# Linear attention of a two-layer step: two output pieces ahead of tile 0, three levels copied by ScalarE, decode preparation on GpSimd

## The reference

```python
def step(S, inp):                       # one chunk of tokens
    qb, kb, vb, gb = inp
    b = jnp.cumsum(gb, axis=2)
    o_inter = jnp.einsum('bhtk,bhkv->bhtv', qb * jnp.exp(b), S)
    decay = jnp.exp(jnp.where(causal, b[:, :, :, None, :] - b[:, :, None, :, :], -jnp.inf))
    att = jnp.einsum('bhtsk,bhsk->bhts', qb[:, :, :, None, :] * decay, kb)
    o_intra = jnp.einsum('bhts,bhsv->bhtv', att, vb)
    b_last = b[:, :, -1:, :]
    S = jnp.exp(b_last[:, :, 0, :])[..., None] * S + jnp.einsum('bhsk,bhsv->bhkv', kb * jnp.exp(b_last - b), vb)
    return S, o_inter + o_intra
...
y = jnp.concatenate([ya, yb, yc], axis=-1) @ lw['w_out']
```

## Time and profile before

| | us |
|---|---|
| median of 3 runs | 2597.96 (2595.11 to 2601.43) |
| the profiled execution, its own time | 2599.04 |
| span of the profiled execution | 2597.2 |
| stage 3 of the first layer, 423.97 to 522.60 | 98.6 |
| stage 3 of the second layer, 1717.80 to 1816.35 | 98.6 |

### The profile page before, as it was taken

One profiled execution on the slowest core, in us unless ns is written; L12 is line 12 of the kernel. 1 busy time (PEld: TensorE's weight loads), 2 busy tenths in 40 slices (PEclk: granted clock), 3 DMA queues, 4 the chain that ended last, 5 costly groups with the idle time before them and its releaser, 6 DMA issues.

```text
span 2597.2 us, 38234 instructions
## 1 busy us (share of the span) xinstructions
PE 2401.4 (92%) x15944; PEld 1422.5 (55%) x15944; DVE 1143.3 (44%) x2122; ACT 689.8 (27%) x1452; POOL 468.2 (18%) x566
## 2 busy tenths in 40 slices
PE   8999998899999999999899999888989999999984
PEld 5645556666666765333366445566666676733332
DVE  3355556843241445333253555568431433633334
ACT  1034444432111331111130344544321123311113
POOL 6004223410100001111260042243100000011112
PEclk9999999999999999999999999999999999999996
DMA  5001001152224228999840010011522421589996
GB/s 187 11 19 30 11 5 38 42 197 92 89 90 148 82 90 310 396 422 422 333 141 11 19 30 11 5 38 44 205 82 65 149 82 65 198 345 406 424 418 244
DMA packets 79220, 389.31 MB, mean 150 GB/s; under 512 B 20654, under 2 KB 24364, under 8 KB 59532
## 3 DMA queue, kind: packets, MB, share of 16 engines
q1 hardware_dynamic: 60892, 308.07, 31.1%
q0 software_dynamic: 17568, 76.57, 7.6%
q10 hardware_dynamic: 576, 2.10, 0.2%
HBM read 354.53 MB, written 41.41 MB: 152 GB/s over the span
## 4 chain that ended last, share of the span: by engine, by line
PE 73%; DVE 11%; ACT 4%; issue 4%; DMA 3%; PEld 2%; POOL 1%; POOLq 0%; PEldq 0%; SPq 0%; DVEq 0%; ACTq 0%
PE ps L1494 12%; PE ps L784 8%; PE ps L807 8%; PE ps L1518 6%; PE ps L1404 4%; PE ps L875 4%; PE ps L955 4%; PE ps L967 3%; PE ps L983 2%; PEld ps L807 2%; PE ps L1160 2%; PE ps L933 2%; DVE arena L2239 2%; PE ps L1480 2%; DMA arena<-yrow 1%
## 5 line engine op out<-in xcount | busy, mean ns | idle before, releaser
L1494 PE MATMUL ps<-arena 128*32 128x512 f32 x2304 | 319.6, 608 | 24.6 <-issue 18.9
L807 PE MATMUL ps<-arena,ring 128*128 128x352 f32 x936 | 283.2, 466 | 1.0 <-ACTq L481 1.0
L784 PE MATMUL ps<-x,ring 128*128 128x352 f32 x768 | 231.5, 463 | 10.6 <-DMA x<-in_x 9.1
L807 PEld LDWEIGHTS ps<-arena,ring 128*128 128x128 f32 x936 | 180.4, 193 | 101.9 <-issue 4.3
L2683 DVE COPY arena<-ps 128x1024 f32<-128x1024 f32 x44 | 53.9, 1224 | 336.9 <-PE ps L1480 336.9
L1494 PEld LDWEIGHTS ps<-arena 128*32 128x32 f32 x2304 | 92.7, 112 | 191.4 <-issue 191.4
L784 PEld LDWEIGHTS ps<-x,ring 128*128 128x128 f32 x768 | 146.8, 192 | 92.7 <-issue 12.8
L1518 PE MATMUL ps<-arena 128*32 128x512 f32 x1408 | 160.2, 595 | 3.8 <-ACT arena L1914 3.8
L2883 POOL DMA_INDIRECT arena<-xrow,arena x46 | 46.8, 1017 | 594.8 <-DVE arena L2658 321.3
L955 PE MATMUL ps<-arena 96*128 96x512 f32 (+3 forms) x384 | 148.7, 497 | 0.0
L1680 ACT ACTIVATE ring<-ps 128x512 f32<-128x512 f32 (+2 forms) x192 | 87.3, 490 | 128.7 <-PE ps L967 128.6
(11 more groups left out here) (471 smaller groups left out, 3836.3 us busy)
## 6 DMA issues: line engine op xcount, KB each, us to landing
arena<-in_w_gu SPq DMA_DIRECT2D x52, 2048.0 KB, 14.3
arena<-in_w_dn SPq DMA_DIRECT2D x64, 1024.0 KB, 11.4
ring<-in_ring SPq DMA_DIRECT2D x56, 512.0 KB, 3.7
ring<-in_w_gu SPq DMA_DIRECT2D x12, 2048.0 KB, 13.7
arena<-yrow SPq DMA_DIRECT2D x16, 1024.0 KB, 9.3
arena<-in_mem_k SPq DMA_DIRECT2D x16, 512.0 KB, 7.6
arena<-in_mem_v SPq DMA_DIRECT2D x16, 512.0 KB, 9.5
xrow<-arena SPq DMA_DIRECT2D x16, 512.0 KB, 7.7
```

Source lines behind the costliest of these rows:

```text
L784: mm = pe.matmul(ps[:, PIECE_BANKS[n % len(PIECE_BANKS)], 0:CH], ring[:, j % RING, k, :], x[:, k, tok], start=k == 0, stop=k == KT - 1)
L807: mm = pe.matmul(ps[:, (j % 2) * NCH + c, 0:CH], ring[:, j // per, (j % per) * units + k, :], src[:, k, tok], start=k == k0, stop=k == uni ...
L1494: mm = pe.matmul(ps[r, 2 + n % 2, :], xb_t[:, n % 2, k, r], w_gu[e % NW][:, k, :], start=k == 0, stop=k == KT - 1, skip_group_check=True)
```

## The change

- **Parts.** Part 0 and part 1 both stand ahead of `levels(0)`. Their weights (both use ring 1) come into a buffer of their own, `w_first`, loaded in stage 2. Part 2 stands between `levels(0)` and `levels(1)`, parts 3 to 7 in tiles 0, 1, 2, 3 and 5. The `keep_clock` of 10 and of 14 go; that of 12 stays.
- **Levels.** DVE's `take_levels` takes the levels 8, 4, 2 and 1 by COPY_PREDICATED. The levels 64, 32 and 16 are plain rectangles, and ACT copies them in seven instructions (`keep_levels`: one, two and four), after `at_free`; then it counts `at_kept`, for which PE's `levels(n + 1)` and `outputs(n)` wait too.
- **State.** `states(n)` makes four products, one a head, so that bank 7 holds only what belongs to the state (cleared once ahead of tile 0), and `add_state` has one instruction in place of two. The turned keys go to the other half of the bank.
- **Start.** DVE runs `begin(2)` ahead of tile 0, once POOL has done the first part of tile 0 (`g_pool` 1), and then `add_part(0)` and `add_part(1)`. ACT runs `decay_exps(2)` there too.
- **Decode tokens.** The running sum, differences, keys and queries are made by POOL behind its tile 7, in buffers of their own; ACT's four exponentials for them stand in tile 7, ahead of `head_squares(7)`. The first cache load comes behind them. DVE's block goes.

```diff
+PART_AT = (0, 1, 2, 3, 5)
...
+                sp.wait_ge(tp_done, SLOT[PAIRS - 2, ("a", 1, 0)] + 1)
+                sp.dma_start(w_first, ins["ring"][l, 2 * RING + PART[0][0]][:, 0:PART_K, :]).then_inc(w_full[0], 16)
...
                     if n >= 1:
                         pe.wait_ge(at_free, n)
+                        pe.wait_ge(at_kept, n)
...
                     pe.wait_ge(kt_evac, n + 1)
-                    pe.matmul(ps[:, 7, 0:GW], g_ktt[:, n % 2, :], vg[:, n, 0:GW], start=True, stop=True).then_inc(st_done, 1)
+                    for h in range(GH):
+                        r, v = slice(GK * h, GK * (h + 1)), slice(GV * h, GV * (h + 1))
+                        mm = pe.matmul(ps[r, 7, v], g_ktt[:, n % 2, r], vg[:, n, v], start=True, stop=True)
+                    mm.then_inc(st_done, 1)
...
-                    pe.wait_ge(ring_full[j], ring_count(l, 3))
+                    if i <= 1:
+                        pe.wait_ge(w_full[0], 16 * (PAIRS // 2 + 1))
+                    else:
+                        pe.wait_ge(ring_full[j], ring_count(l, 3))
                     if i >= 1:
                         pe.wait_ge(part_or_counts_ready, i)
...
-                keep_clock(5, 10)
                 part(0)
+                part(1)
                 levels(0)
-                part(1)
+                part(2)
...
-                    if n == 0:
-                        pe.wait_ge(part_or_counts_ready, 2)
-                        keep_clock(5, 14)
-                    if 1 <= n <= len(PART) - 3:
-                        part(1 + n)
+                    if n in PART_AT:
+                        part(3 + PART_AT.index(n))
...
+                def keep_levels(n):
+
+                    act.wait_ge(at_free, n + 1)
+                    for lv, z in enumerate(LEVELS[:HIGH]):
+                        for b in range(HALF // z):
+                            s_, at = 2 * z * b, lv * HALF + z * b
+                            last = act.activation(g_att[s_:s_ + z, n % 2, :, s_ + z:s_ + 2 * z], ps[s_:s_ + z, 0:GH, at:at + z], ACT.Copy)
...
-                    for lv, z in enumerate(LEVELS):
+                    for lv, z in list(enumerate(LEVELS))[HIGH:]:
...
-                    step(dve.tensor_tensor(g_tmp, ps[:, bank, 0:GW], bd, ALU.mult))
-                    dve.scalar_tensor_tensor(out=dst, in0=dst, scalar=scale, in1=g_tmp, op0=ALU.mult, op1=ALU.add).then_inc(st_ready, 1)
+                    dve.scalar_tensor_tensor(out=dst, in0=dst, scalar=scale, in1=ps[:, bank, 0:GW], op0=ALU.mult, op1=ALU.add).then_inc(st_ready, 1)
...
+                dve.wait_ge(g_pool, 1)
+                begin(2)
                 add_part(0)
+                add_part(1)
```

More of the change, by code:

```diff
@@ L271, in build @@
         la_t = view(SC + 3072 + TOK, TOK)
-        NL = len(LEVELS)
+        NL, HIGH = len(LEVELS), 3
         HALF = P // 2
@@ L286, in build @@
         d_e, d_k = view(PR, 3, ND), view(PR + 96, 3, ND)
+        d_b, d_eb, d_ek, d_kt0, d_qe0 = (view(S2 + 1280 + ND * k, ND) for k in range(5))
+        d_last = view(S2 + 1280 + 5 * ND, DB)
         d_q0, d_q = view(PR + 192, GH, ND), view(PR + 320, 2, GH, ND)
@@ L413, in build @@
         row_moved = [sem(f"row_moved{j}") for j in range(4)]
-        wg_full = [(sem(f"wg_full{j}"), 0) for j in range(4)] + [(w_full[0], 16 * PAIRS // 2)]
+        wg_full = [(sem(f"wg_full{j}"), 0) for j in range(4)] + [(w_full[0], 16 * (PAIRS // 2 + 1))]
         wd_full = [(s, 32 * PAIRS) for s in swap_or_dn_full] + [(w_full[1], 16 * PAIRS // 2)]
@@ L1109, in _ @@
                         turn_o(n - 2)
-                part(len(PART) - 1)
                 pe.wait_ge(g_dve, 1)
@@ L1738, in take_kt @@
                     act.wait_ge(kt_done, n + 1)
-                    act.activation(g_ktt[0:w, n % 2, :], ps[0:w, 7, 0:P], ACT.Copy).then_inc(kt_evac, 1)
+                    act.activation(g_ktt[0:w, n % 2, :], ps[0:w, 7, GW:GW + P], ACT.Copy).then_inc(kt_evac, 1)
+                def keep_levels(n):
[4 more added lines that the diff above has]
+                            last = act.activation(g_att[s_:s_ + z, n % 2, :, s_ + z:s_ + 2 * z], ps[s_:s_ + z, 0:GH, at:at + z], ACT.Copy)
+                            if at + z < HIGH * HALF:
+                                step.mark(last)
+                    last.then_inc(at_kept, 1)
                 def head_squares(n, w):
@@ L1759, in _ @@
                     state_exps(n)
+                decay_exps(2)
+                keep_levels(0)
                 for n in range(NT):
-                    if n + 2 < NT:
+                    if n >= 1 and n + 2 < NT:
                         decay_exps(n + 2)
@@ L1769, in _ @@
                         act.wait_ge(o_root, n // 2)
+                    if n + 1 < NT:
+                        keep_levels(n + 1)
+                    else:
+                        act.wait_ge(g_sub, NT + 1)
+                        step.mark(act.activation(d_e[:, 0:2, :], d_e[:, 0:2, :], ACT.Exp))
+                        step.mark(act.activation(d_eb, d_b, ACT.Exp))
+                        step.mark(act.activation(d_ek, d_ek, ACT.Exp))
+                        act.activation(d_last, d_b.rearrange("p (b t) -> p b t", b=DB)[:, :, DT - 1], ACT.Exp).then_inc(g_exp, 1)
                     head_squares(n, P)
@@ L2280, in _ @@
                     if n == 0:
-                        add_part(1)
+                        add_part(2)
                     if n >= 1:
@@ L2290, in _ @@
                         norm_o(n - 2, P)
-                    if 2 <= n <= len(PART) - 2:
-                        add_part(n)
+                    if n - 1 in PART_AT:
+                        add_part(3 + PART_AT.index(n - 1))
                 dve.wait_ge(st_done, NT)
```

86 lines of the change are left out of this document (42 added, 44 removed).

## The result

The changed kernel takes 2617.28 us (median of 6 runs, 2611.43 to 2624.09). The kernel before, in runs on the same chip, takes 2596.53 (6 runs, 2587.59 to 2603.88). The ratio is 1.0079, with an interval of 1.0064 to 1.0095: slower by 0.8%, where 2597.6 and a range up to 2606 had been forecast. Even the slowest rival, 2606.6, is 10.7 us short of it. The profiled execution took 2619.86 us with a span of 2618.0, against 2599.04 and the span of the earlier trace rows: +20.8.

A forecast was written before the change was run, and what follows sets the result against it. The prediction took DVE to set the loop's pace, with PE close behind. Head +9.3, loop -5.4 and tail -4.1 summed to -0.2 us a layer, -0.4 in two, for a median of 2597.6 us, range 2590 to 2606.

The forecast's parts named there:

- Head, +9.3: Stage 3 to the end of tile 0's levels: part 1 waits for add_part(0), clock falls; +9.3 us a layer.
- Tail, -4.1: Behind tile 7's levels: decode outputs start at +13.8 us and not +17.9; -4.1 us a layer.
- Loop, -5.4: From tile 0's levels to tile 7's: seven steps sum to 53.1 us against 58.5; -5.4 us a layer.
- chain of 7.6: One tile of the loop: DVE levels, L2240, add_state, state_exps, ACT's copies at 1.4, PE's levels, in series; 7.6 us.
- slower rival (c): In keep_levels: ACT's copies set the pace, seven take 2.1 us, 4 to 5 us a layer more, 2606.6 us; chance 15%.
- point of decision, 1.8: Time of ACT's seven copies in keep_levels, about 1.8 us, from which the slower rival (c) decides.

The follow-up runs named there:

- h1: Changed kernel with add_part(0) on DVE moved ahead of the wait for g_pool and begin(2): 2608.60 us, ratio 1.0064.
- b3: Changed kernel with only add_part(0) moved on DVE ahead of begin(1), no warming products added: 2596.15 us, ratio 1.0000.
- w1: Changed kernel with warming products put back: 26 between parts 0 and 1, 5 at the start of pass 0, 16 in pass 4: 2601.92 us, ratio 1.0023.
- hw2: Changed kernel with add_part(0) ahead of begin(2) and warming products: 18 behind part 1, 5 in pass 0, 16 in pass 4: 2599.40 us, ratio 0.9995.
- c1: Kernel before the change without its 24 warming products (ten ahead of part 0, fourteen in tile 0): 2604.07 us, ratio 1.0034.
- k1: Changed kernel with ACT's level copies ahead of the root and the state's exponentials: 2614.69 us, ratio 1.0074.
- hwk2: Kernel of hw2 with ACT's level copies ahead of the root and the state's exponentials: 2601.65 us, ratio 1.0021.
- ws0: Kernel of w1 with DVE copying all seven levels again and no wait for at_kept: 2596.41 us, ratio 1.0001.
- b2: Kernel of b1 with DVE copying all seven levels again: 2590.42 us, ratio 0.9975.
- b1: Changed kernel with add_part(0) on DVE ahead of begin(1), and warming products in passes 0 and 4, none in the head: 2581.92 us, ratio 0.9944.

## Why the prediction was wrong, step by step

- **Head, +9.3: right** (+10.2 and +9.7), by the mechanism told. POOL's product ended 8.9 us into the stage (8.3 forecast), the sum and the subtractions took 0.66 and 2.41 (0.4 and 2.1), the clock cost part 1 2.3 us (2.5). h1 and b3 show that the order of `add_part(0)` and `begin(2)` is the cause.
- **Tail, -4.1: right** (-3.7), term by term: exponentials done at +8.1 (+7.5), POOL hidden, outputs at +14.4 (+13.8), 11.6 behind them as before.
- **Loop, -5.4: wrong** (+4.3, +3.6). The step that failed is that every step of the loop was priced at full clock, with the sentence "The 24 warming products that go were no cost: tile 0's 14 stood in a wait for DVE". w1 and hw2 give what the clock cost the new loop, 6.8 to 6.9 us: some 2.7 in the step to tile 2, where the fourteen had stood, and 4.25 in the steps to tiles 6 and 7, behind the wait of the pass that no longer has a part. That the fourteen stood in a wait is true, but not that they were no cost to lose: c1 gives the price of the 24 in the kernel before, 4.3 us a layer, of which 3.3 and 2.7 in the loop. The rows for it were at hand: the earlier trace rows showed the clock falling after a rest of PE, and the prediction used this for the head alone. It priced the wait of the pass without a part as time, not as a rest that lets the clock fall.
- **The other 2.9 us** are terms of the loop that were too small, by w1's steps at full clock: the first 6.98 (6.4), tiles 2 to 4 7.95 (7.5), tile 5 8.77 (8.5), tile 6 8.24 (7.6), tile 7 8.14 (8.1). The largest common part is ACT's seven copies, 1.77 and not 1.4, because they don't overlap: the forecast's own chain of 7.6 with 0.37 more is 7.97, and tiles 2 to 4 came at 7.95, though the forecast had put PE's 7.5 there. Where the copies stood outside of the chain (k1, hwk2) those steps were 7.46 to 7.47.
- **The slower rival (c)** gave 2606.6 and stood closest to the result, but not for its reason. It needed copies of 2.1 us; they took 1.77, just under its point of decision, 1.8. In the steps to tiles 3 and 4 of the changed kernel PE does wait 0.42 and 0.43 us for them, but ws0 and b2, which have no copies on ACT and kept the clock, are no faster in the loop.
- **The size of it**: 6.85 + 2.9 = 9.7 us in layer 1 is what the loop missed by. With the head's +0.9 and the tail's +0.4 that makes 11.0 a layer, the difference between the forecast -0.2 and the +10.8 measured. (The forecast read the end of the low stretch in the earlier trace rows as 515.6; a clock of 0.70 in 515.50:516.00 puts it at 515.8. Nothing hangs on it.)

## What to carry to other kernels

A batch of products that computes nothing is not free to delete because it stands in a wait; ask what the clock does in that wait without it, and price every later step at both clocks. When work is moved ahead on one engine, move what it feeds from on the other engines too: one DVE instruction that stood behind a group waiting for GpSimd cost 8 to 9 us a layer. Moving work off the busiest engine brought nothing here, where another engine's own cycle, 7.5 us of PE, lies just under it and the moved work lands in series (loops of 55.9 to 56.1 us at full clock either way).

## What the runs showed of the hardware

- **The clock fell within loops in which PE rested only briefly.** Ahead of the levels of tile 1 of the changed kernel PE rested 1.22 us, worked on, and the clock fell at 446.2. In the second layer of the kernel before it fell at 1734.4, behind a rest of 0.83 us; after one of 0.85 us at the same place of the first layer it did not. The Trainium skill, TensorE: Matmul & The Clock Gate, section Part 1, says that the throttled state is the default and is released by activity; the clock's return under dense work (453.0, 497.4) agrees. What exactly lets it fall behind so short a rest, these runs do not show.
- **Whether it falls depends on the layer and the execution.** The same code kept it up in layer 1 of w1 (step of 8.24) and lost it in layer 2 (10.66); h1 lost it in the step to tile 2 in layer 1 (10.71) and kept it in layer 2 (7.94). That section says the same of slow products at a kernel's start, whose number varies between runs of one kernel. So one profiled execution doesn't price an edit of this kind, as the table shows for h1 and b1.
- **At 0.5 PE's instructions took nearly twice as long**: the levels 3.26 us against 1.79, the eight products of the outputs at L1068 1.81 against 1.00; a part (twelve records) that lay partly or wholly in a low stretch took 5.2 to 6.8 against 3.8.
- **Narrow copies out of PSUM got little cheaper and did not overlap on ACT**: 0.214 us for 16 partitions by 64, 0.364 for 64 by 256, four times the elements in each partition; seven in a row took 1.76 to 1.78 where their lengths add up to 1.74.
- **A switch of table cost its load and no more**: 1.28 us, with 0.02 us to the instruction on either side (482.42 and 483.72). The Trainium skill, ScalarE: Activation LUTs, section What ACT_TABLE_LOAD costs, gives the same 1283 ns and another 1.38 us to drain; no such gap is in these rows, and the measurement decides.
